# Encoder kernel on one core: the opening's bias replication, value products and root table, and the channel order of the norms

## The reference, cut to what matters

```python
def rms_norm(x, g):
    y = xf * lax.rsqrt(jnp.mean(xf * xf, axis=-1, keepdims=True) + RMS_EPS)
    return (y * g.astype(jnp.float32)).astype(x.dtype)
...
for layer in range(DEPTH):                       # DEPTH = 2
    hp = rms_norm(xp, norm_mix[layer]); hs = rms_norm(xs, norm_mix[layer])
    if layer % 2 == 0:   # q, k, v = h @ w_qkv; softmax(q k^T * scale + bias[q_pos - k_pos]) v; x += o @ w_o
    else:                # pointwise D->2D, GLU, causal conv of 31 taps, LayerNorm, swish, pointwise D->D
    # then, in every layer: top-1 of 4 groups, top-2 of its 8 experts, gated MLP of width 256
    xp = xp + hier_moe(rms_norm(xp, norm_ffn[layer]), ...)
```

## Time and profile before

| | us |
|---|---|
| median of 3 runs | 1431.17 (1425.56 to 1433.93) |
| the profiled execution | 1430.13 |
| its span in the trace | 1428.4 |
| TensorE granted clock, mean | 0.887 of full |

### The profile page before, as it was taken

One profiled execution on the slowest core, in us unless ns is written; L12 is line 12 of the kernel. 1 busy time (PEld: TensorE's weight loads), 2 busy tenths in 40 slices (PEclk: granted clock), 3 DMA queues, 4 the chain that ended last, 5 costly groups with the idle time before them and its releaser, 6 DMA issues.

```text
span 1428.4 us, 14655 instructions
## 1 busy us (share of the span) xinstructions
PE 1145.4 (80%) x5278; PEld 612.6 (43%) x5278; DVE 546.7 (38%) x1088; ACT 263.5 (18%) x591; POOL 93.4 (7%) x131
## 2 busy tenths in 40 slices
PE   4999999988884977887727999995974987778870
PEld 3777777764443322222204555553433322222320
DVE  3133333342436111111124899996446111111115
ACT  3123232231101111111013212204101111111002
POOL 1000000000014000000020000000003100000003
PEclk8999999987985998898966999997986898999995
DMA  9943333516016899999956511100005999999956
GB/s 200 276 125 98 97 97 97 207 50 262 38 59 236 352 422 422 421 421 422 417 166 221 211 57 31 29 1 22 0 29 185 381 423 422 423 423 422 422 220 228
DMA packets 106806, 322.75 MB, mean 226 GB/s; under 512 B 12643, under 2 KB 59763, under 8 KB 81777
## 3 DMA queue, kind: packets, MB, share of 16 engines
q1 hardware_dynamic: 94465, 288.18, 53.0%
q0 software_dynamic: 12304, 34.09, 6.7%
HBM read 270.36 MB, written 61.84 MB: 233 GB/s over the span
## 4 chain that ended last, share of the span: by engine, by line
PE 56%; DMA 26%; DVE 10%; SPq 4%; issue 3%; ACT 1%; POOL 0%; DVEq 0%; POOLq 0%
DMA ring<-in_w_up 23%; PE bank L1038 11%; PE bank L1308 8%; PE bank L479 8%; PE bank L396 7%; PE bank L506 4%; SPq L792 3%; PE bank L1321 3%; PE bank L1311 2%; PE bank L527 2%; PE bank L1055 2%; PE bank L543 2%; PE bank L568 2%; DMA ring<-y_sorted,slot 1%; DVE ring L1431 1%
## 5 line engine op out<-in xcount | busy, mean ns | idle before, releaser
L1038 PE MATMUL bank<-ring,work 128*64 128x512 f32 x1056 | 279.6, 690 | 74.9 <-DMA ring<-in_w_up 71.6
L1038 PEld LDWEIGHTS bank<-ring,work 128*64 128x64 f32 x1056 | 90.9, 158 | 261.1 <-issue 219.1
L1070 DVE TENSOR_TENSOR work<-work,bank 128x256 f32<-128x256 f32 x33 | 20.0, 607 | 342.6 <-ACT work L1066 342.6
L1431 DVE SCALAR_TENSOR_TENSOR ring<-work,ring 128x606 f32<-128x606 f32 x192 | 146.7, 845 | 0.0
L1055 PE MATMUL bank<-ring,work 128*64 128x512 f32 x528 | 122.3, 605 | 20.6 <-DVE work L1075 20.6
L479 PE MATMUL bank<-xt_flat,ring 128*128 128x288 f32 x512 | 135.9, 421 | 0.6 <-ACT xt_flat L333 0.6
L396 PE MATMUL bank<-ring,xn_flat 128*128 128x512 f32 x256 | 122.2, 632 | 7.4 <-ACT xn_flat L1398 6.6
L1308 PE MATMUL bank<-xt_flat,work 128*128 128x512 f32 x256 | 113.6, 602 | 0.6 <-issue 0.6
L479 PEld LDWEIGHTS bank<-xt_flat,ring 128*128 128x128 f32 x512 | 97.4, 195 | 34.6 <-issue 7.7
L396 PEld LDWEIGHTS bank<-ring,xn_flat 128*128 128x128 f32 x256 | 50.6, 204 | 65.6 <-issue 64.5
L1308 PEld LDWEIGHTS bank<-xt_flat,work 128*128 128x128 f32 x256 | 48.8, 193 | 59.3 <-issue 59.3
(11 more groups left out here) (223 smaller groups left out, 1151.9 us busy)
## 6 DMA issues: line engine op xcount, KB each, us to landing
ring<-in_w_gate SPq DMA_DIRECT2D x32, 2048.0 KB, 19.8
ring<-in_w_up SPq DMA_DIRECT2D x32, 2048.0 KB, 24.3
ring<-in_w_down SPq DMA_DIRECT2D x32, 2048.0 KB, 25.0
work<-x_sorted SPq DMA_DIRECT2D x33, 512.0 KB, 10.2
ring<-in_w_qkv SPq DMA_DIRECT2D x24, 512.0 KB, 5.9
x_sorted<-gain POOLq DMA_DIRECT2D x8, 1536.0 KB, 5.8
y_sorted<-work SPq DMA_DIRECT2D x17, 512.0 KB, 24.3
y_sorted<-gain SPq DMA_DIRECT2D x16, 512.0 KB, 25.4
```

The source lines that it names most:

```text
L1038: mm = nc.tensor.matmul(bank[2 + s][rr, :], xte[s][:, c, rr], wgu[s][:, :, e, c, :], start=c == 0, stop=c == C - 1)
L1431: steps.behind(V.scalar_tensor_tensor(a, src(t), w(t), a, ALU.mult, ALU.add))
```

## The change

- The bias table is loaded first of all DMAs, eight copies of its 16 rows on all 128 partitions. GpSimd, not DVE, extends it (`rel_ext`), and the replication to HBM reads from 128 partitions, 16 rows each, where it read from 16 partitions, 128 rows each.
- SP issues the value weights first, then q and k, then the replication, and only behind it `kcache` and the V cache rows; then it waits for `rel_out` and issues the bias read, and behind it the weights of pair 1 and `w_o`. In the loop the load of pair n+2 waits for `small_mm` as well.
- PE does the value products of tile j-1 after the transposes of tile j, into banks 3 and 4. The projection of pair 0 is then q0, q1, k0, k1, kc.
- The masking memset moves from DVE to GpSimd. GpSimd writes the constants `eps` first; ACT takes one root of them at once, which loads its table.
- Norms and the experts' hidden product write channels in their natural order; the transposes read every eighth value, 32 bytes apart (every second one of the hidden row), so that the chunks stay the same. The final norm was in natural order already.

```diff
-        xn_cp = xn_flat[:].rearrange("p (j c q) -> p j q c", j=TILES, c=C)
+        xn_pc = xn_flat[:].rearrange("p (j q c) -> p j c q", j=TILES, c=C)
...
+        xe_pc = [a.rearrange("p (q c) -> p c q", c=C) for a in xe]
...
-        hid_cp = hid.rearrange("p (c q) -> p q c", c=FC)
+        hid_pc = hid.rearrange("p (q c) -> p c q", c=FC)
...
-            nc.vector.scalar_tensor_tensor(out, src, ss[0:r, 2, j:j + 1], g, ALU.mult, ALU.mult).then_inc(normed, 1)
+            out = (xf if n % 2 else xn)[0:r, j, :]
+            nc.vector.scalar_tensor_tensor(out, x[0:r, j, :], ss[0:r, 2, j:j + 1], gain[0:r, 0, :], ALU.mult,
+                                           ALU.mult).then_inc(normed, 1)
...
-                mm = nc.tensor.transpose(b[:, (c % 4) * P:(c % 4) * P + r], src[0:r, j, c * P:(c + 1) * P],
+                mm = nc.tensor.transpose(b[:, (c % 4) * P:(c % 4) * P + r], src[0:r, j, c, :],
                                          ident[0:r, 0:r])
...
-            pe.wait_ge(turn_ev_a, TILES)
-            pe.wait_ge(turn_ev_d, TILES)
+            def first_value(j):
+                pe.wait_ge(turn_ev_a, j + 1)
+                pe.wait_ge(turn_ev_d, j + 1)
+                if j == 0:
+                    pe.wait_ge(wv_in, 16)
+                    pe.sem_inc(wa_in[0], 16)
...
+                for c in range(C):
+                    mm = nc.tensor.matmul(out, xt_tile(c, j), wa[0][:, 2, c, :], start=c == 0, stop=c == C - 1)
...
+            for j in range(TILES):
+                turn_pe(pe, 0, j)
+                if j >= 1:
+                    first_value(j - 1)
+            first_value(TILES - 1)
...
-            for piece in ("q0", "q1", "k0", "k1", "kc", "v0", "v1", "v4"):
+            for piece in ("q0", "q1", "k0", "k1", "kc"):
...
-            sp.dma_start(bias_rows.rearrange("r h m -> h r m"),
-                         rel_sb[0:HEADS, 0:EXT].unsqueeze(1).to_broadcast([HEADS, P, EXT])).then_inc(rel_out, 16)
+            sp.dma_start(bias_rows.rearrange("(i c) h m -> (c h) i m", c=COPIES),
+                         rel_sb[:, 0:EXT].unsqueeze(1).to_broadcast([P, P // COPIES, EXT])).then_inc(rel_out, 16)
+            sp.dma_start(kcache[:, 0, :], heads2d(cache_attn_k[0, 0])[:, 0:P]).then_inc(wa_in[0], 16)
             load_v(0, 0)
+            sp.wait_ge(rel_out, 16)
...
+                    sp.wait_ge(small_mm, n + 1)
                     sp.wait_ge(v4_mm, n + 1)
                     load(n + 2, s)
...
-            nc.vector.tensor_tensor(hid_cp, sg.rearrange("p (q c) -> p q c", c=FC),
-                                    bank[2 + s][:, FE:2 * FE].rearrange("p (q c) -> p q c", c=FC), ALU.mult).then_inc(m.hid, 1)
+            nc.vector.tensor_tensor(hid, sg, bank[2 + s][:, FE:2 * FE], ALU.mult).then_inc(m.hid, 1)
...
+            pool.wait_ge(rel_in, 16)
+            pool.tensor_copy(rel_sb[:, 0:P - 1], rel_sb[:, P - 1:P].to_broadcast([P, P - 1])).then_inc(rel_ext, 1)
...
+            nc.scalar.activation(warm[:], eps[:], ACT.Sqrt)
```

More of the change, by code:

```diff
@@ L82, in encoder @@
     OUTS = SPAN - STATE
+    COPIES = P // HEADS
     STEPS = TILES
@@ L116, in encoder @@
         eps = sb("eps", [P, 1])
+        warm = sb("warm", [P, 1])
         ln_eps = sb("ln_eps", [P, 1])
@@ L239, in encoder @@
         dve_steps = sem("dve_steps"); act_steps = sem("act_steps"); pool_steps = sem("pool_steps")
-        wa_in = [sem(f"wa_in{s}") for s in range(2)]; vc_in = [sem(f"vc_in{s}") for s in range(2)]
+        wv_in = sem("wv_in"); wa_in = [sem(f"wa_in{s}") for s in range(2)]; vc_in = [sem(f"vc_in{s}") for s in range(2)]
         q_mm = sem("q_mm"); k_mm = sem("k_mm"); small_mm = sem("small_mm"); v_mm = sem("v_mm"); v4_mm = sem("v4_mm")
@@ L303, in norm_dve @@
             wait_x(dve, n, j)
-            final = n == 2 * LAYERS
-            out = xn[0:r, j, :] if final else (xf_cp if n % 2 else xn_cp)[0:r, j, :, :]
-            src = x[0:r, j, :] if final else x[0:r, j, :].rearrange("p (q c) -> p q c", c=C)
-            g = gain[0:r, 0, :] if final else gain[0:r, 0, :].rearrange("p (q c) -> p q c", c=C)
-            nc.vector.scalar_tensor_tensor(out, src, ss[0:r, 2, j:j + 1], g, ALU.mult, ALU.mult).then_inc(normed, 1)
+            out = (xf if n % 2 else xn)[0:r, j, :]
+            nc.vector.scalar_tensor_tensor(out, x[0:r, j, :], ss[0:r, 2, j:j + 1], gain[0:r, 0, :], ALU.mult,
+                                           ALU.mult).then_inc(normed, 1)
         TURN_BANKS = ((0, 1), (2, 7))
@@ L608, in pair @@
                 values(n, s, k, 4)
-            pe.wait_ge(turn_ev_a, TILES)
-            pe.wait_ge(turn_ev_d, TILES)
+            def first_value(j):
[4 more added lines that the diff above has]
+                    pe.sem_inc(wa_in[0], 16)
+                last = j == TILES - 1
+                out = bank[4][0:DEC, 0:P] if last else bank[3][:, j * P:(j + 1) * P]
+                for c in range(C):
+                    mm = nc.tensor.matmul(out, xt_tile(c, j), wa[0][:, 2, c, :], start=c == 0, stop=c == C - 1)
+                if j >= TILES - 2:
+                    mm.then_inc(v4_mm if last else v_mm, 1)
+            for j in range(TILES):
[3 more added lines that the diff above has]
+            first_value(TILES - 1)
             pe.wait_ge(consts, CONSTS)
-            for piece in ("q0", "q1", "k0", "k1", "kc", "v0", "v1", "v4"):
+            for piece in ("q0", "q1", "k0", "k1", "kc"):
                 project(0, 0, 0, piece)
+            pe.wait_ge(v_ev, 1)
+            pe.wait_ge(v4_ev, 1)
             with pe.Fori(0, PAIRS // 2 - 1) as it:
@@ L764, in attn_dve @@
                 dve.sem_inc(begins_free, FREE)
+            value_copy(0, 0, 0, 3)
+            value4_copy(0, 0, 0, 4)
             for h in range(2):
                 key_copy(0, 0, h)
-            value_copy(0, 0, 0)
-            value4_copy(0, 0, 0)
-            dve.wait_ge(bias_in, 16)
-            V.memset(bias[0:CHUNK, :, WIN - CHUNK:WIN], -BIG).then_inc(bias_masked, 1)
             dve.wait_ge(bias_masked, 1)
@@ L832, in store @@
                     pool.dma_start(heads2d(dst)[KEEP - DEC:KEEP, cols(n)], src).then_inc(kv_out[s], 16)
+            pool.wait_ge(bias_in, 16)
+            pool.memset(bias[0:CHUNK, :, WIN - CHUNK:WIN], -BIG).then_inc(bias_masked, 1)
             zeros = lambda a: gain[:, 1, :].unsqueeze(1).to_broadcast([P, a, D])
@@ L1512, in _ @@
             steps = Steps(pool, pool_steps)
+            steps.done(pool.memset(eps[:], 1e-6))
+            steps.done(pool.memset(ln_eps[:], 1e-5))
+            pool.sem_inc(consts, 1)
             for t, fill, cmp, pat, mult, b in ((ident, 1.0, ALU.not_equal, [[-1, P]], 1, 0),):
```

42 lines of the change are left out of this document (18 added, 24 removed).

## The result

| | before | after |
|---|---|---|
| median, us | 1429.01 (4 runs, 1425.56 to 1433.93) | 1409.33 (4 runs, 1408.44 to 1410.40) |
| the profiled execution | 1430.13 | 1410.40 |
| its span | 1428.4 | 1408.7 |
| TensorE granted clock, mean | 0.887 | 0.893 |

The ratio of after to before is 0.9856, with a 95% interval of 0.9835 to 0.9877: 1.4% faster, some 20 us, where 13.6 were forecast. 1409.33 lies in the predicted range (1408 to 1427), at its lower end, and outside the forecast's own range (1413 to 1422). It is the time that rival (a) gave together with the fast replication, 1409, and not that of the forecast, 1417.5. The gain has the places that the forecast named, and two of its terms have other sizes.

What follows compares the result with a forecast made beforehand. The prediction took the experts as DMA-bound at about 422 GB/s, the head pairs as PE-bound and the opening as held by the late bias. 1430.1 - 11.0 - 8.0 + 6.4 = 1417.5 us, 8-in-10 range 1408 to 1427.

Steps and rivals of the forecast that it cites:

- rival (a): PE's transposes: strided reads cost nothing, giving 1411 us, or 1409 with 422 GB/s replication; chance 0.22.
- the fast replication: Opening: bias replication to HBM at 422 GB/s, so PE's own end at 29 us binds and 13.4 us are gained.
- The replication: Opening: copying the bias to HBM from 128 partitions at 292 GB/s takes 10.7 us, kcache landing at about 30.2.
- The opening's sum: Start to pair 1's first filled-in piece: 85.1 us in place of 96.14, 11.0 us gained.
- Values: Opening: 9.3 us of pair 0's value products move from behind k to ahead of q, where PE is mostly free.
- Natural order on DVE: Norms and hidden product written in natural order: 3.5, 4.1 and 0.4 us gained, together 8.0 us.
- Strided reads on PE: Transposes reading with a stride: 1.53 times the load time, 0.5 us per warm group, 6.4 us given back.
- the prediction's own sign: One strided PE weight load of L321 and L1049 at full clock: 0.11 us if free, 0.16 forecast, 0.21 if doubled.
- rival (b): PE's transposes: strides double every weight load or more, 11.4 us given back at twice, so 1422.5 us; chance 0.16.
- the forecast's 8.0: Gain in us from natural channel order in DVE's norms and the experts' hidden product.
- The other signs: Profile after: replication landing within 15 us, no DVE wait for bias, experts' stages unchanged to a microsecond, router stages not growing.

Runs made afterwards that it cites:

- e7: Changed kernel with all of pair 0's value products back behind the K cache's turn, fast replication kept: 1417.96 us, ratio 0.9930 to the kernel before.
- e5: Changed kernel with the replication read from 16 partitions again: 1429.69 us, ratio 0.9998 to the kernel before.
- e8: Changed kernel with the root table loaded behind all tiles of x, still on 128 partitions and extended by GpSimd: 1404.58 us, ratio 0.9834 to before.
- e1: Changed kernel with norms, transposes and hidden product as before, so the new opening alone: 1417.38 us against 1430.09, ratio 0.9912.
- e3: Changed kernel whose PE transposes read 128 neighbouring values, so chunks hold wrong channels: 1404.89 us, ratio 0.9846 to the kernel before.
- e2: Kernel before with only the natural channel order and its strided transposes added: 1420.02 us against 1430.09, ratio 0.9933.
- e6: Changed kernel with the replication from 16 partitions and pair 0's kcache issued ahead of it: 1427.72 us, ratio 0.9980 to the kernel before.
- e9: Changed kernel with 26 identity transposes ahead of PE's first group and 8 ahead of the first values: 1405.52 us, ratio 0.9842 to before.
- e11: Changed kernel with added identity transposes, value weights issued behind x's second tile, kcache ahead of the replication: 1403.63 us, ratio 0.9833 to before.

## Why the prediction was right or wrong

**The replication.** The prediction's step said 292 GB/s, with `kcache` at 30.2 and q0 waiting for it. The profile shows 358 GB/s, the replication done by 29.6 and q0 at 30.12 with no idle time. `kcache` lands 15.1 us after its issue at 14.97, so at 30.1; 28.8 is where it lets q0 go in e7. PE's own end was put at 29 to 30 and came at 30.1. So the arrival came as forecast, but from two errors that cancel: at 358 GB/s the 3.14 MB take 8.8 us and not 10.7, which puts their beginning (an estimate) at 20.8 and not at 19.2. That the 16 source partitions, and not the length of the rows in HBM, 1532 bytes in both, made the old 109 GB/s, e5 shows, save that the order of the rows written changes too: the same bytes from 16 partitions land 34.6 us after the issue. The half of "Door 1: The DMA port swizzle" in the Trainium skill (SBUF — State Buffer) that the earlier trace rows could not show is borne out in its direction: 128 partitions are over three times as fast. The 436 GB/s that it gives for them are not reached in this stretch.

**The opening's sum.** 11.0 us were forecast, 13.1 are measured at pair 1's piece. The price given for a fast replication was 13.4; its own terms, 29 + 16.3 + 1.2 = 46.5, make it 13.9. The term that was too large: as PE does not stop ahead of q0, q and k take 15.76 us in place of the 18.04 that I carried over from the earlier trace rows. e7, where PE stops 7.36 us there, has the 18.61 again. The bias was no wait afterwards, and pairs 1 and 2 keep 35.7 us, as predicted.

**Values.** Moved as forecast into time in which PE stood, and worth 10.8 us in e7. The early root table by itself is worth nothing (e8), so what frees the norms is that DVE no longer copies the table. The prediction took the table's early load for part of the cause of the first transposes at 9 us; they come at 8.26 without it.

**Natural order on DVE.** The norms themselves are sized right: L307 is at 1.28 to 1.31 us everywhere, and in n = 2 the stretch from the first addition of the combine on DVE to the convolution's first product is 769.97 - 744.34 = 25.6 us before and 751.74 - 729.26 = 22.5 after, 3.2 gained for 3.5 forecast. In n = 1 and 3 it was 4.1 us forecast, and the chains gain 1.2 and 1.4. From each of the first two norms in that chain to the product that waits behind it are 3.2 us before and 2.6 after, 0.6 gained for 0.69; but the products behind take longer, in n = 1 9.23 us for 8.96 and 9.15 for 8.72. They start at half clock, and in the third and fourth us behind their start the granted clock is 0.52 and 0.68 before, and 0.50 in both after. In the experts of the two layers the chains gain 1.8 and 2.5 us where 0.2 each were forecast; layer 0's is the earlier rise of the clock in the first product for the most part, and layer 1's e1 has without the natural order.

**Strided reads on PE.** The step that failed, by size. "The nearest row of the trace is what a stride costs DVE", 1.53 times, gave 6.4 us back. The listed load does grow by a third (146 to 195 ns in the mean), but a load runs beside the transpose before it, and a group of eight takes 1.16 us for 1.09, or 0.88 for 0.87 in the chain; a cold one takes 1.99 for 1.98. Over the forecast's eight warm groups that is 0.1 to 0.6 us, and the 64-row group of the opening, which the prediction let lie beside the wait for `kcache`, adds 0.4, so the term is about 1 us or less. By the prediction's own sign, an eighth of the eight warm loads is 0.97 / 8 = 0.12 us, next to the 0.11 of rival (a) and not the 0.16 of the forecast. The factor of 1.5 was right for the one group where the load sets the pace, 1.09 us against 0.71. The rule on lines of 16 bytes (the Trainium skill, Advanced Engine Details and Errata, "SBUF Cachelines"), on which rival (b) drew, is right that the read itself suffers; but the read sets the pace only in that 64-row group. Rival (b)'s 11.4 us are excluded by e3, which gives PE its contiguous reads back and gains 1.4 us by the ratios (0.9846 against 0.9856, each inside the other's interval).

**The sum again.** With the opening as measured, an estimated 0.5 us for the strides and the forecast's 8.0 kept: 1430.1 - 13.1 - 8.0 + 0.5 = 1409.5, against 1410.4 for the profiled execution. That this closes is in part luck, for the 8.0 was nowhere measured as such: e2 gives 9.6 to 10.1 by time, and the chain behind pair 1's piece 19.7 - 13.1 = 6.6, with the convolution's +2.7 and the -2.5 of layer 1's experts in it, neither of which an experiment ties to the order of the channels. The two terms that missed, 2.1 us in the opening and 6 in the strides, both missed to the same side, and the range held because it reached to rival (a).

**The other signs.** The replication landed 16.5 us after its issue, where 15 was the sign. DVE did not wait for the bias, as forecast. The experts' stages are 1.8 and 2.5 us shorter, where they were to keep their length to a microsecond. The router stages did not grow.

## What to carry to other kernels

A DMA between SBUF and HBM that moves many bytes out of few partitions is a suspect even while the DMA engines look busy; put the copies on all partitions first, and ask what stands behind it in the queue, for e6 shows that moving one victim forward only brings the next. Put a rearrangement where it is hidden: here the strided side cost DVE 0.69 us each time on the critical path, and PE, whose loads run beside its transposes, next to nothing where those have 128 rows, and 0.38 us for a group where they have 64 and the clock is full. And take work that has its data into a known wait, but look at which arrival is next: in e9 PE was ready 2.2 us before `kcache` was.

## What the runs showed of the hardware

**Listed loads and the pace.** A strided weight load of 128x128 fp32 values is listed at 195 ns in the mean where the contiguous one has 146, while the transposes around it keep 296 against 289. A longer listed load is not yet a longer group: it becomes one in the 64-row tile, 1.09 us for 0.71. The two transposes of the hidden row, whose values lie 8 bytes apart, take 0.50 us in most pairs for 0.44 in e3. On DVE, results that go 512 bytes apart cost 1.98 us for 1.29.

**PE's clock at the start.** 26 transposes of the identity over 4.85 us, ended 2.3 us ahead of the first real group, left that group at 1.97 us in e9. In e11 the same 26 took 5.32 us and ended 1.9 us ahead, and the group took 1.31:

```profile
9.34 1.31 PE L321 MATMUL bank<-ident,xn_flat 128*128 128x128 f32 x8 [1.91 <-DVE xn_flat L307]
```

Which of the two differences decides was not tested. The view of stretches for e9 (us, busy time of each engine, granted clock, DMA share, GB/s) has this:

```profile
7.00:11.30 4.30, 1.97 (x8) 1.57 (x8) 2.06 (x4) 2.09 (x7) 3.41 (x14) 0.76 1.05 399
11.30:15.40 4.10, 3.19 (x15) 3.19 (x16) 3.50 (x5) 3.08 (x6) 1.44 (x3) 0.50 1.14 222
15.40:18.00 2.60, 2.60 (x21) 2.28 (x20) 1.45 (x2) 0.74 (x3) 0.00 (x0) 0.87 1.09 358
```

In e9 the clock falls to 0.50 of full (1.2 GHz) and is back at 2.4 GHz only behind the eight transposes that run without a gap into the values. In the kernel after the same stretches list a granted clock of 1.00, though their groups take 1.94 and 1.97 us as well. In these first microseconds the duration of a known group tells the clock, and the listed one does not.

**The same code, other times.** From the first piece on, six kernels with the same instructions took between 1356.4 and 1362.2 us in their profiled runs. An edit worth 2 us in the opening can be seen in the trace and not in the time.
